# The passage from the gate stage to the dense stage: a first small store, eight early gathers, and the split of the token halves in the last routing head

## The chip, the cores and the metric

The kernel runs on one core of a Trainium2 chip. The metric is the device time of one execution in microseconds (us). A time `t` is counted from the start of the profiled execution's span. Engines: TensorE (PE, and PEld for its weight loads), VectorE (DVE), ScalarE (ACT), GpSimd (POOL), and SyncE (SP), which only issues DMAs here. Sixteen DMA engines serve two queues: q1, fed by SP, and q0, fed by GpSimd's indirect DMAs.

## The reference

Two layers over 640 tokens (512 latent, 128 context) of width 1024. Layer 0 mixes tokens by grouped-query attention, layer 1 by pooling. Each mixer is followed by a PEER channel mixer, which is where the change lies:

```
q  = (x @ wq) -> (t, 8 heads, 2 halves, 128);  sc = q . keys           # 128 keys per half
s_top, i_top = top_k(sc, 16)
cs, ci = top_k(s_top[0][:, None] + s_top[1][None, :], 16)              # 16 of 256 pairs
idx = i1 * 128 + i2;   g = softmax(cs)                                 # 16384 experts
act = gelu(u[idx] . x, exact) * g;   out = sum_k act_k * v[idx_k]      # per token: 8 x 16 experts
```

u and v have 16384 rows of 1024 numbers each, per layer, in float32.

## The kernel before, in words

**Two ways for the experts.** The 640 tokens are five tiles of 128. For three tiles (384 tokens, `TD`) the experts are computed densely: all 128x128 experts, 128 "key rows" q of 128 experts each, with a gate matrix that is zero where a token did not choose an expert. For the other two tiles (256 tokens, `NG`) the rows of u and v that each token chose are gathered by indirect DMA, 128 rows of 4 KB (0.524 MB) at a time, 256 of them in u and 256 in v per layer, and VectorE does the products. Both ways run at the same time, in the dense stage. "Expert q" below is such a key row of 128 experts.

**Stages of a layer's channel mixer.** (1) Routing: TensorE and ScalarE produce the scores of 16 half-heads; VectorE takes the top 16 head by head (`routing`, some 25.6 us a head); GpSimd multiplies and folds the masks of each head (lines 464 to 476). After the eighth head come the softmax of the gates, the row numbers `idx` (line 930) and the low half of the dense tokens, `hl = hT - hh` (line 933), where `hh` is ScalarE's rounding of `hT` (line 532). (2) Gate stage: three blocks of 128 tokens. For each, TensorE transposes the picks, VectorE copies them to `pickT` (942) and builds one-hot tiles `hot` for four tokens at a time (952), GpSimd multiplies one of the two by the gates (487), TensorE multiplies the pair (1106) and ScalarE copies the result to `gbuf` (541). `gbuf` has two halves of 64 tokens; SP stores each full half, 4 MB, into the scratch tensor `gates_d` in HBM (`store_gates`, 362), six stores per layer. (3) Dense stage, 16 groups of eight experts (`experts` on each engine): per expert a scan on TensorE (24 matmuls, lines 1118 to 1120: u in a high and a low half, `uh` and `ul`, against `hh` and `hl`), gelu on ScalarE (560), the product with the gate on VectorE (989, from `gp`, four key rows read back from `gates_d`), splits of v and of that product (`vh`, `vl`, `wh`, `wl`), and a spread on TensorE (18 matmuls, 1130 to 1132). TensorE runs scan q+1 ahead of spread q. Beside it VectorE does four gathered rows per expert: in the first eight groups dot products with u rows against the tokens `htok` (`u_row`, 970), in the last eight sums of v rows into `acc` (`v_row`, 979).

**The order around the change.** Every engine has its instructions in one fixed order. Between the last gate copy and the first scan: TensorE transposes the gathered tiles' tokens into PSUM, ScalarE splits two u tiles and then waits for the semaphore `dense_begun`. VectorE raises `dense_begun` (1008) only when both halves' last stores have landed (`stored[0]`, `stored[1]`), then clears `acc` (1009). Behind `dense_begun` stand: SP's loads, in the order gates 0 to 3, v pairs 0 and 1, gates 4 to 7; ScalarE's copies of `htok` (576); GpSimd's first gather (506). The ring of gathered rows has eight buffers (`rows`), free again when VectorE has used one. In the loop SP issues, per pair p of experts, `load_u(p+2)` when `ul` of that slot is made, `load_v(p+2)` when `vl` is, and every second pair the gates. The buffers of the dense stage overlay those of the routing and gate stages in SBUF, which is why the gathers and some loads wait for the stores.

## Time and profile before

| | us |
|---|---|
| median of three runs | 3490.77 (3490.72 to 3492.78) |
| the profiled execution's own time | 3486.53 |
| its span, first to last instruction | 3484.7 |
| TensorE busy (matmuls) | 3144.4 (90%) |
| VectorE busy | 2939.8 (84%) |
| GpSimd busy | 1897.1 (54%) |
| ScalarE busy | 1053.9 (30%) |
| DMA, mean over the span | 286 GB/s |

Busy times overlap, so they do not add up to the span. A mean share mixes stages: in the dense stages (t=801 to 1889 and 2367 to 3455) TensorE, VectorE and the DMA engines are all near full, in the routing stages only VectorE is. The granted TensorE clock is given as a share of full speed (1.00 is 2.4 GHz, 0.50 is 1.2 GHz). In a timeline row, the bracket at the end gives the idle time of the engine just before the row and what ended it.

### The profile page before, as it was taken

What the parts mean: (1) busy time and instruction counts of PE and PEld (TensorE: products, weight loads), DVE (VectorE), ACT (ScalarE), POOL (GpSimd) and SP (SyncE); (2) the same over time, 40 slices, a digit from 0 to 9 for tenths busy, and PEclk for the clock granted to TensorE, in tenths of its full rate; (3) what the DMA queues carried; (4) which work ended last, traced back from release to release, by engine and by line L of the source; (5) the groups of instructions that cost most, each with busy time, mean ns of one, the idle gap of its engine ahead of it and who ended that gap; (6) DMA issues with size and microseconds to landing.
All of it is one profiled execution on the core that took longest, in us unless ns stands there. A gap on an engine that the chain in (4) does not pass through costs nothing.

```text
span 3484.7 us, 50069 instructions
## 1 busy us (share of the span) xinstructions
PE 3144.4 (90%) x15686; PEld 2594.2 (74%) x15686; DVE 2939.8 (84%) x5453; ACT 1053.9 (30%) x1587; POOL 1897.1 (54%) x1412
## 2 busy tenths in 40 slices
PE   5988999398999999999998597298999999999997
PEld 3555555277999999899987264277999999999996
DVE  1655278897999999999998678896999999999998
ACT  2122111143333333333333210143333333333332
POOL 0000023485777887777774023485777777676673
PEclk8999999699999999999999798599999999999999
DMA  5122154048999999999997010048999999999995
GB/s 200 49 98 74 73 189 174 24 199 348 410 408 407 404 402 380 402 404 406 402 387 282 24 49 0 24 205 350 409 409 408 403 404 395 410 401 404 407 400 204
DMA packets 244633, 995.72 MB, mean 286 GB/s; under 512 B 22608, under 2 KB 72528, under 8 KB 204880
## 3 DMA queue, kind: packets, MB, share of 16 engines
q0 software_dynamic: 147456, 536.94, 39.0%
q1 hardware_dynamic: 97104, 457.82, 33.4%
q8 instruction: 45, 0.74, 0.1%
q14 instruction: 28, 0.23, 0.0%
HBM read 941.45 MB, written 53.22 MB: 285 GB/s over the span
## 4 chain that ended last, share of the span: by engine, by line
PE 64%; DVE 18%; issue 8%; DMA 7%; POOL 2%; ACT 1%; DVEq 0%; POOLq 0%; SPq 0%; ACTq 0%
PE bankA L1118 7%; PE bankA L1120 7%; PE bankA L1119 7%; PE bankD L1106 6%; PE bankD L1131 5%; PE bankD L1132 5%; PE bankD L1130 5%; PE bankA L1210 5%; DMA rows<-in_v,idxc 4%; DVE acc L979 3%; PE bankA L1132 2%; PE bankA L1131 2%; PE bankA L1130 2%; PE bankD L1256 2%; DMA rows<-in_u,idxc 1%
## 5 line engine op out<-in xcount | busy, mean ns | idle before, releaser
L506 POOL DMA_INDIRECT rows<-in_u,idxc x512 | 750.2, 1465 | 235.1 <-issue 129.4
L506 POOL DMA_INDIRECT rows<-in_v,idxc x512 | 688.0, 1344 | 252.1 <-issue 134.1
L1118 PE MATMUL bankA<-hh,uh 128*128 128x384 f32 x2048 | 689.8, 337 | 22.5 <-ACT htok L576 13.8
L1120 PE MATMUL bankA<-hh,ul 128*128 128x384 f32 x2048 | 689.6, 337 | 0.0
L1119 PE MATMUL bankA<-hl,uh 128*128 128x384 f32 x2048 | 688.2, 336 | 0.0
L979 DVE SCALAR_TENSOR_TENSOR acc<-rows,a,acc 128x1024 f32<-128x1024 f32 x512 | 634.6, 1278 | 15.9 <-DMA rows<-in_v,idxc 15.4
L970 DVE CUSTOM_DVE_ANT_0 rows<-rows,htok 128x1024 f32<-128x1024 f32 x512 | 607.1, 1219 | 21.0 <-DMA rows<-in_u,idxc 19.7
L468 POOL TENSOR_TENSOR mask<-mask,topf 128x1280 f32<-128x1280 f32 x32 | 91.9, 2893 | 875.0 <-DVE mask L898 875.0
L560 ACT ACTIVATE wt<-bankA 128x384 f32<-128x384 f32 x256 | 126.0, 492 | 971.7 <-PE bankA L1120 971.6
L1118 PEld LDWEIGHTS bankA<-hh,uh 128*128 128x128 f32 x2048 | 386.4, 189 | 34.5 <-ACT htok L576 14.5
L1131 PE MATMUL bankD<-vl,wh 128*128 128x512 f32 x1024 | 400.0, 391 | 0.0
L1132 PE MATMUL bankD<-vh,wl 128*128 128x512 f32 x1024 | 399.4, 390 | 0.0
L1130 PE MATMUL bankD<-vh,wh 128*128 128x512 f32 x1024 | 398.6, 389 | 0.0
L1210 PE MATMUL bankA<-hT,wch 128*128 128x512 f32 (+1 forms) x1344 | 377.9, 440 | 22.1 <-ACT hT L621 21.8
L1119 PEld LDWEIGHTS bankA<-hl,uh 128*128 128x128 f32 x2048 | 386.1, 189 | 9.7
L1120 PEld LDWEIGHTS bankA<-hh,ul 128*128 128x128 f32 x2048 | 385.9, 188 | 0.0
L1210 PEld LDWEIGHTS bankA<-hT,wch 128*128 128x128 f32 x1344 | 209.6, 194 | 191.2 <-issue 188.4
L991 DVE TENSOR_TENSOR vl<-vraw,vh 128x1024 fp32r<-128x1024 f32 x256 | 312.3, 1220 | 32.2 <-ACT vh L564 31.7
L963 DVE TENSOR_TENSOR ul<-uraw,uh 128x1024 fp32r<-128x1024 f32 x256 | 311.8, 1219 | 9.2 <-ACT uh L550 9.2
L564 ACT CAST vh<-vraw 128x1024 fp32r<-128x1024 f32 x256 | 266.5, 1041 | 11.6 <-DMA vraw<-in_vP 11.6
L550 ACT CAST uh<-uraw 128x1024 fp32r<-128x1024 f32 x256 | 268.6, 1050 | 0.0
L566 ACT CAST wh<-wt 128x384 fp32r<-128x384 f32 x256 | 131.4, 513 | 403.9 <-DVE wt L989 403.7
(178 smaller groups left out, 4589.9 us busy)
## 6 DMA issues: line engine op xcount, KB each, us to landing
uraw<-in_uT SPq DMA_DIRECT2D x128, 1024.0 KB, 16.2
vraw<-in_vP SPq DMA_DIRECT2D x128, 1024.0 KB, 7.9
gates_scratch<-gbuf SPq DMA_DIRECT2D x12, 4096.0 KB, 11.6
gp<-gates_scratch SPq DMA_DIRECT2D x64, 768.0 KB, 16.3
sq<-in_ada SPq DMA_DIRECT2D x14, 2048.0 KB, 8.0
wch<-in_ada SPq DMA_DIRECT2D x10, 2048.0 KB, 8.0
wch<-in_wq SPq DMA_DIRECT2D x8, 2048.0 KB, 8.1
rows<-in_u,idxc POOLq DMA_INDIRECT x512, 9.8
```

The lines of the kernel that those rows point to most:

```text
L506: pool.indirect_dma_start(out=rows[:, j, :], out_offset=None, in_=table.rearrange("l e d -> (l e) d"), in_offset=bass.IndirectOffsetOnAxis ...
L963: v.tensor_tensor(ul[:, c, :], uraw[:, b, c * D:(c + 1) * D], uh[:, c, :].bitcast(F32), ALU.subtract).then_inc(ul_ready, 1)
L970: v.tensor_tensor_reduce(out=rows[:, r % RING, :], in0=rows[:, r % RING, :], in1=htok[:, r % GT, :], scale=1.0, scalar=0.0, op0=ALU.mult, ...
L979: v.scalar_tensor_tensor(out=acc[:, r % GT, :], in0=rows[:, r % RING, :], scalar=a8[:, r:r + 1], in1=acc[:, r % GT, :], op0=ALU.mult, op1= ...
L991: v.tensor_tensor(vl[:, c % 2, :], vraw[:, b, c % 2 * D:(c % 2 + 1) * D], vh[:, c % 2, :].bitcast(F32), ALU.subtract).then_inc(vl_ready, 1)
L1118: pe.matmul(abank[c], hi, hh[:, k, :], start=k == 0, stop=False)
L1119: pe.matmul(abank[c], hi, hl[:, k, :], start=False, stop=False)
L1120: last = pe.matmul(abank[c], lo, hh[:, k, :], start=False, stop=k == K - 1)
L1130: pe.matmul(y, hi, vh[:, c, a:a + 512], start=first, stop=False)
L1131: pe.matmul(y, hi, vl[:, c, a:a + 512], start=False, stop=False)
L1132: last = pe.matmul(y, lo, vh[:, c, a:a + 512], start=False, stop=final)
L1210: last = pe.matmul(bank[:, a:b], w[:, k, (c % 4) * P:(c % 4 + 1) * P], hT[:, k, a:b], start=k == 0, stop=k == K - 1)
```

## The change

Four edits.

1. `hl` is computed by GpSimd instead of VectorE, between the seventh and the eighth head's masks. ScalarE makes `hh` before it waits for the softmax, and TensorE transposes the gathered tiles' tokens (`htok`) before it waits for the gates; ScalarE's copies follow at once.
2. The last block's second half is stored in two parts: its first eight key rows (256 KB, semaphore `edge_stored`), and the rest later. `dense_begun` waits for the copies into `gbuf` and for the first half's store alone. SP's order becomes: first part of the store, v pair 0, (wait for the first part) gates 0 to 3, v pair 1, rest of the store, u pair 2, (wait for the rest) gates 4 to 7, and on as before.
3. GpSimd issues the first eight gathers in the gate stage: three after block 1, three after block 2, two after block 3. For this five of the eight row buffers lie over `hT` and three in a tile of their own, and other dense tiles change places.
4. `acc` is cleared between the u rows and the v rows, in the middle of the dense stage.

```diff
@@ SBUF
-            hh = sb("hh", [P, K, TD], F32R, where=dn)
-            hl = sb("hl", [P, K, TD], F32R, where=dn)
+            htok = sb("htok", [P, GT, D], where=dn)
             uraw = sb("uraw", [P, 2, 2 * D], where=dn)
+            rowsB = sb("rowsB", [P, RING - TILES, D], where=dn)
...
-            rows = sb("rows", [P, RING, D], where=dn)
-            htok = sb("htok", [P, GT, D], where=dn)
-            acc = sb("acc", [P, GT, D], where=dn)
+        hrows = hT[:, :, :].rearrange("p k t -> p (k t)").rearrange("p (r d) -> p r d", d=D)
+        row_buf = [hrows[:, j, :] if j < TILES else rowsB[:, j - TILES, :] for j in range(RING)]
+        htok_bank = [bankA[0], bankD[1]]
@@ SP
-                    sp.dma_start(gates_d[b], gbuf[:, b % 2, :, :]).then_inc(stored[b % 2], 16)
+                    if b < TD // TB - 1:
+                        sp.dma_start(gates_d[b], gbuf[:, b % 2, :, :]).then_inc(stored[b % 2], 16)
+                    else:
+                        sp.dma_start(gates_d[b][:, 0:GROUP, :], gbuf[:, b % 2, 0:GROUP, :]).then_inc(edge_stored, 16)
+
+            def store_rest(L):
+
+                b = TD // TB - 1
+                sp.dma_start(gates_d[b][:, GROUP:NKEY, :], gbuf[:, b % 2, GROUP:NKEY, :]).then_inc(stored[b % 2], 16)
...
                             load_u(L, g * (GROUP // 2) + (p + 2), p % 2)
+                            if first and p == 0:
+                                sp.wait_ge(stored[1], 16 * ((L + 1) * DT + 1))
+                                load_gates(4, 1)
...
                 sp.wait_ge(dense_begun, L + 1)
+                load_v(L, 0, 0)
+                sp.wait_ge(edge_stored, 16 * (L + 1))
                 load_gates(0, 0)
-                load_v(L, 0, 0)
                 load_v(L, 1, 1)
-                load_gates(4, 1)
-                with sp.Fori(0, GROUPS - 1) as g:
+                store_rest(L)
+                group(0, first=True)
+                with sp.Fori(1, GROUPS - 1) as g:
                     group(g)
@@ GpSimd
+                with pool.Fori(0, PH - 1) as h:
+                    pick_keys(h)
+                pool.wait_ge(split_h, L + 1)
+                pool.tensor_tensor(hl[:, :, :], hT[:, :, 0:TD], hh[:, :, :].bitcast(F32), ALU.subtract
+                                   ).then_inc(h_split, 1)
+                pick_keys(PH - 1)
+                pool.wait_ge(idx_ready, L + 1)
+                pool.wait_ge(h_split, L + 1)
+                pool.wait_ge(htok_full, (L + 1) * GT)
+                pool.tensor_copy(idxc[:, 0, :], idx[:, 0:RING]).then_inc(idx_copied, 1)
...
+                for i in range(1, DT + 1):
                     pool.wait_ge(pickT_ready, i + L * DT)
...
                                 ALU.mult).then_inc(hotg_ready, 1)
-                pool.wait_ge(idx_ready, L + 1)
-                pool.wait_ge(dense_begun, L + 1)
...
+                    for j in range(3 * i - 3, min(3 * i, RING)):
+                        gather(u_d, j, 0)
@@ ScalarE
+                act.copy(hh[:, :, :], hT[:, :, 0:TD]).then_inc(split_h, 1)
+                for j in range(GT):
+                    act.wait_ge(htok_full, L * GT + j + 1)
+                    act.copy(htok[:, j, :], htok_bank[j][:, :]).then_inc(htok_ready, 1)
                 act.wait_ge(gexp_in, L + 1)
@@ VectorE
-                v.wait_ge(split_h, L + 1)
-                v.tensor_tensor(hl[:, :, :], hT[:, :, 0:TD], hh[:, :, :].bitcast(F32), ALU.subtract).then_inc(h_split, 1)
...
+                v.wait_ge(g_out, (L + 1) * DT * (P // HOT) + 2)
+                v.wait_ge(stored[0], 16 * ((L + 1) * DT + 1))
+                v.sem_inc(dense_begun, 1)
                 for c in range(2):
                     split_u(L * NKEY + c, 0, c)
-                v.wait_ge(g_out, (L + 1) * DT * (P // HOT) + 2)
-                for i in range(2):
-                    v.wait_ge(stored[i], 16 * ((L + 1) * DT + 1))
-                v.sem_inc(dense_begun, 1)
-                then(v.memset(acc[:, :, :], 0.0))
...
                 v.sem_inc(u_done, 1)
+                v.wait_ge(stored[1], 16 * ((L + 1) * DT + 1))
+                then(v.memset(acc[:, :, :], 0.0))
@@ TensorE
+                pe.wait_ge(a_free, BEFORE[L])
+                pe.wait_ge(sc_copied, HP * (L + 1))
+                for j in range(GT):
+                    for m in range(K):
+                        last = pe.transpose(htok_bank[j][:, m * P:(m + 1) * P], hT[:, m, (DT + j) * P:(DT + j + 1) * P], ident)
+                    last.then_inc(htok_full, 1)
                 pe.wait_ge(routed, L + 1)
```

## Rows read from the trace of the kernel before

**Rows 1.** Stretches: length, busy us (instructions) by engine, granted clock, DMA share, GB/s.
```profile
801.00:850.00 49.00, 34.85 (x166) 30.63 (x164) 25.49 (x35) 14.86 (x20) 21.94 (x20) 0.90 0.92 369
850.00:900.00 50.00, 49.46 (x250) 44.93 (x251) 48.58 (x75) 17.38 (x24) 34.94 (x27) 1.00 1.03 407
...
1369.00:1889.00 520.00, 517.37 (x2605) 468.47 (x2603) 500.79 (x506) 177.92 (x247) 377.77 (x277) 1.00 0.99 389
```
**Rows 2.** TensorE's waits, 801 to 870: total us, times, longest.
```profile
PE bankA L1118 <- ACT htok L576: 6.9, 1, 6.9
PE bankA L1118 <- DVE ul L963: 5.2, 3, 3.0
PE bankA L1130 <- DVE wl L994: 2.6, 2, 1.8
```
**Rows 3.** The chain of waits over both passages: start us, us, what.
```profile
800.76 13.04 DMA gates_scratch<-gbuf
...
829.30 18.70 DMA rows<-in_u,idxc
...
850.54 0.41 PE bankA L1118
...
2367.34 13.04 DMA gates_scratch<-gbuf
...
2416.57 0.41 PE bankA L1118
```
**Rows 4.** The same chain, end of layer 0's routing.
```profile
672.49 3.27 DVE hl L933
675.75 0.22 DVE bankA L937
```
**Rows 5.** Timeline, GpSimd's masks of head 6 and ScalarE's softmax exponent.
```profile
631.27 5.72 POOL L468 TENSOR_TENSOR mask<-mask,topf 128x1280 f32<-128x1280 f32 x2 [16.69 <-DVE mask L898]
...
668.61 0.74 ACT L530 ACTIVATE gt<-gt 128x640 f32<-128x640 f32 x1 [47.78 <-DVE gt L917]
```
**Rows 6.** Timeline of layer 0's passage.
```profile
803.29 2.36 DVE L963 TENSOR_TENSOR ul<-uraw,uh 128x1024 fp32r<-128x1024 f32 x2 [3.52 <-ACT uh L550]
...
813.98 1.01 ACT L576 COPY htok<-bankA 128x1024 f32<-128x1024 f32 x1 [9.85 <-DVEq L1008]
...
814.50 1.76 DVE L1009 MEMSET acc<- 128x2048 f32 x1 [8.85 <-DMA gates_scratch<-gbuf]
...
819.05 0.56 DVE L989 TENSOR_TENSOR wt<-wt,gp 128x384 f32<-128x384 f32 x1 [2.78 <-DMA gp<-gates_scratch]
...
821.89 1.05 ACT L564 CAST vh<-vraw 128x1024 fp32r<-128x1024 f32 x1 [5.59 <-DMA vraw<-in_vP]
...
824.81 0.47 PE L1130 MATMUL bankA<-vh,wh 128*128 128x512 f32 x1 [1.76 <-DVE wl L994]
```
**Rows 7.** Timeline, first work after the change from block 1 to block 2.
```profile
720.96 4.42 POOL L487 TENSOR_TENSOR hot<-hot,pickT 128x512 f32<-128x512 f32 x4 [4.42 <-DVE hot L952]
...
722.05 3.20 PE L1106 MATMUL bankD<-hot 128*128 128x128 f32 x16 [3.98 <-POOL hot L487]
```
**Rows 8.** A stretch behind that idle time, columns as in rows 1.
```profile
724.00:726.00 2.00, 2.00 (x11) 2.00 (x11) 1.72 (x3) 0.78 (x2) 1.81 (x3) 0.50 1.22 524
```
**Rows 9.** DMA issues of the page: count, KB each, us to landing.
```profile
out_yT<-hT SPq DMA_DIRECT2D x8, 320.0 KB, 2.4
```
**Rows 10.** DMA queues in 822 to 830: packets, MB, share of 16 engines.
```profile
q0 software_dynamic: 557, 2.02, 63.6%
q1 hardware_dynamic: 551, 1.20, 38.8%
```
**Rows 11.** Line 506, the gathers' issue on GpSimd: ns min/median/max.
```profile
L506 POOL DMA_INDIRECT rows<-in_u,idxc x512: 937/1307/1992, 815.6 to 2906.9; - x171
L506 POOL DMA_INDIRECT rows<-in_v,idxc x512: 934/1202/4019, 1343.3 to 3437.1; - x171
```
**Rows 12.** Timeline, VectorE between the u rows and the v rows.
```profile
1355.24 0.45 DVE L1020 TENSOR_TENSOR actg<-actg,gate 128x256 f32<-128x256 f32 x1 [0.80 <-ACT actg L581]
```

More of the change, by code:

```diff
@@ L213, in build @@
                     sq = sb("sq", [P, K, T], where=wide)
-                with ExitStack() as gb:
-                    pickT = sb("pickT", [P, 3, P], where=gb)
-                    hot = sb("hot", [P, SLOTS, 2, HOT, P], where=gb)
-                    gbuf = sb("gbuf", [P, 2, NKEY, TB], where=gb)
             QT, OT = qT[:, 0:NH, :], qT[:, NH:2 * NH, :]
@@ L237, in build @@
                 gsum = sb("gsum", [P, TILES * PH], where=rt)
+                pickT = sb("pickT", [P, 3, P], where=rt)
+                hot = sb("hot", [P, SLOTS, 2, HOT, P], where=rt)
+                gbuf = sb("gbuf", [P, 2, NKEY, TB], where=rt)
             with ExitStack() as pl:
@@ L377, in expert_loads, with group @@
             def expert_loads(L):
-                def group(g, last=False):
+                def group(g, first=False, last=False):
                     for p in range(GROUP // 2):
@@ L477, in _, with gather, gather_ring @@
                     last.then_inc(mask_done, 1)
-                with pool.Fori(1, DT + 1) as i:
+                def gather(table, slot, g):
+                    pool.indirect_dma_start(
+                        out=row_buf[slot], out_offset=None, in_=table.rearrange("l e d -> (l e) d"),
+                        in_offset=bass.IndirectOffsetOnAxis(ap=idxc[:, g % 2, slot:slot + 1], axis=0),
+                    ).then_inc(row_ready[slot], 16)
+                def gather_ring(table, i, it, g):
+                    pool.wait_ge(rows_free, it * ROWS + (g * RING + 1))
+                    rows_of = bass.ds(i * ROWS + g * RING, RING) if not isinstance(i, int) else slice(
+                        i * ROWS + g * RING, i * ROWS + (g + 1) * RING)
+                    pool.tensor_copy(idxc[:, g % 2, :], idx[:, rows_of]).then_inc(idx_copied, 1)
+                    pool.wait_ge(idx_copied, it * (ROWS // RING) + (g + 1))
+                    pool.sem_inc(pool_passed, 1)
+                    for j in range(RING):
+                        pool.wait_ge(rows_free, it * ROWS + (g * RING + j + 1))
+                        pool.sem_inc(pool_passed, 1)
+                        gather(table, j, g)
+                with pool.Fori(0, PH - 1) as h:
[8 more added lines that the diff above has]
+                pool.tensor_copy(idxc[:, 0, :], idx[:, 0:RING]).then_inc(idx_copied, 1)
+                pool.wait_ge(idx_copied, L * 2 * ITERS * (ROWS // RING) + 1)
+                pool.wait_ge(rows_free, L * 2 * ITERS * ROWS + RING)
+                for i in range(1, DT + 1):
                     pool.wait_ge(pickT_ready, i + L * DT)
-                    pool.sem_inc(pool_passed, 1)
                     with pool.Fori(0, P // HOT // SLOTS) as k:
@@ L573, in experts @@
                 act.wait_ge(dense_begun, L + 1)
-                for j in range(GT):
-                    act.wait_ge(htok_full, L * GT + j + 1)
-                    act.copy(htok[:, j, :], ybank[j][:, :]).then_inc(htok_ready, 1)
                 with act.Fori(0, ITERS) as g:
@@ L1140, in group @@
                         spread(q, c % 2, first and c == 0, last and c == GROUP - 1)
-                for j in range(GT):
-                    for m in range(K):
-                        last = pe.transpose(ybank[j][:, m * P:(m + 1) * P], hT[:, m, (DT + j) * P:(DT + j + 1) * P], ident)
-                    last.then_inc(htok_full, 1)
                 pe.wait_ge(h_split, L + 1)
```

47 lines of the change are left out of this document (23 added, 24 removed).

## The prediction

> **What bounds the kernel now.** I read the stretches table first, then TensorE's waits, then the chain of waits over the two passages, and last the timeline around each edited step. Each layer has a routing stage on VectorE, a gate stage (three blocks of 128 tokens), and a dense stage of 128 experts that takes some 1060 of the layer's 1700 us. In the dense stage TensorE is busy 517.4 of 520 us in the second half of layer 0, while the 16 DMA engines are busy 0.99 of that time at 389 GB/s, and 1.03 at 407 GB/s in the 50 us after t=850 [rows 1]. So the body is set by TensorE with DMA right behind it; 2605 matmuls in 517.4 us are 0.199 us each, and the 42 of one expert (24 of the scan, 18 of the spread) take 8.3 us. Nothing in the change touches this body. What it touches is the way in: between t=801 and 850 TensorE is busy 34.9 of 49 us. Its waits there are 6.9 us for the token copy htok, 5.2 us for ul and 2.6 us for wl [rows 2]. The chain says what stands behind them: the last 4 MB gate store takes 13.04 us from t=800.76, with everything held behind it, and then the first row gathers arrive late (18.70 us for one), so that the scan of expert 4 starts at 850.54, 49.8 us after the last store's issue. In layer 1 it is 2367.34 to 2416.57, 49.2 us [rows 3]. From there on TensorE hardly stops. The start of scan 4 is therefore my landmark: what the change wins up to there, it keeps, if DMA lets it.
>
> **Part 1, the token halves.** Before, the split's difference hl is on the chain for 3.27 us on VectorE, between the expert numbers and the gate stage [rows 4]. It moves to GpSimd, ahead of the last head's masks. GpSimd idles 16.69 us before each head's masks and does a 1280-element pair product in 2.86 us (5.72 for two) [rows 5]; 3072 elements at that rate are 6.9 us. It starts when head 6's masks are done and fits more than twice, so even a doubled price costs nothing. Its input, ScalarE's copy hh, and the two htok copies (1.01 us each) move into the 47.78 us for which ScalarE stood idle before the softmax exponent [rows 5]. TensorE's 16 transposes for htok go into its idle time there as well. Gain 3.3 us a layer, all on the chain; what is late next is pickT, which waits for nothing else. If the cover were gone, each us of excess over 16.7 would cost one.
>
> **Part 2, the passage.** I keep the trace's own times and take the 3.3 us off at the end. Unchanged: the casts uh on ScalarE, then ul on VectorE at 803.29 (two in 2.36 us), so scan 0 starts at 804.66 [rows 6]. TensorE then has been idle since 800.2, 4.5 us, because the transposes that stood there are gone. After an idle time of 3.98 us at a block's change [rows 7] the granted clock was 0.50 in 724 to 726, the 1.2 GHz level [rows 8], and about 3.4 us of half speed cost 1.7 us of work. I charge that: scan 0 ends at 804.66+4.15+1.7 = 810.5, scan 1 at 814.65.
> For spread 0 there have to be: the gates of experts 0 to 3, vraw, and the chain gelu, wt, vh, vl, wl. Only 8 key rows (256 KB) are stored first; a 320 KB store lands in 2.4 us [rows 9], so at 803.2. The read-back took 5.0 us (813.98 to 819.05, where wt started as it landed) [rows 6]; with the 1 MB of vraw ahead of it in SP's queue (2.6 us at 407 GB/s) it lands at 810.9. vraw, issued at 801.1, needed 7.5 us before (landed 821.89) [rows 6] and is there at 808.6. Gelu ends at 811.0, then vh 1.05, vl 1.22, wl 0.55: 813.9. So spread 0 starts behind scan 1 at 814.65, against 824.81 before [rows 6].
> From there the experts follow without a gap if the rows are in place: eight are, for experts 0 and 1. Spread 0 ends at 818.8, then scan 2, spread 1, scan 3, spread 2 at 4.15 each: scan 4 at 835.4 against 850.54. That is 15.1 us, the best that TensorE can do.
> The DMA engines give the other bound. From 801 to 850 they moved 49 x 369 = 18.1 MB [rows 1], 4.2 of it the store, so 13.9 MB of dense data by the landmark. Now six gathers (3.15 MB of 0.524 each) came earlier, but 4.2 MB of store go inside: 14.9 MB at 407 GB/s are 36.6 us, plus some 2 us before the first data, from 801: 839.6, 10.9 us won. The need is not strict, since some of the 13.9 MB was ahead of its use. I take the middle of 10.9 and 15.1, 13.0 us.
> SP's queue in this passage: behind its new wait for the rest of the store stand the second gate load, vraw pair 2, then uraw pair 3. The rest (3.9 MB) is issued at about 804 behind 2.8 MB of loads and lands near 824 (its predecessor's 13.04 us from 811). The gates of experts 4 to 7 and vraw pair 2 are needed at 844 and 845, and uraw pair 2, issued ahead of the wait but moved behind the rest, at 833: covered by 7 us or more. If that cover is gone TensorE waits at scan 4.
>
> The trace shows how the two queues share an engine: in 822 to 830 the gathers' queue moved 557 packets and SP's 551, yet 2.02 and 1.20 MB [rows 10]; they alternate by packet, not by byte. The Trainium skill ("DMA: Bandwidth & Descriptors", Queues, rings and completion order) says the same: an engine takes a whole packet from one ring before it goes to the next. The trace agrees. It speaks against this change, as gbuf is stored in runs of 30 KB a partition and a row is 4 KB: by it, gathers issued from 815 on stand nearly still until the store's rest is through near 822, and if that made scan 4 some 2 us later, the sum would be 3464.
>
> **Part 3, gathers in the gate stage.** Eight indirect DMAs go on GpSimd's queue: three after block 1, three after block 2, two after block 3. GpSimd idles 4.42 us at a block's change [rows 7]. An issue lasts 0.94 us at least, 1.31 in the median of the dense stage, plus 0.3 to the next [rows 11]: three are 3.7 to 4.8 us. Two changes cost 0 to 0.4 us each, and I take 0.5 a layer for them and the index copy. The last two follow the last product, where nothing waits. The gathers' own buffers (five of eight now over hT, three behind uraw) wait only for the split and the transposes, long done. The DMA engines were half idle there, so the data is free.
>
> **Part 4, the cleared accumulator.** Its 1.76 us [rows 6] stood in the passage's idle time and go to the middle of the dense stage, ahead of the product with the gate, which waited 0.80 us for ScalarE anyway [rows 12]. VectorE loses 1.0 us once a layer; TensorE had no wait there. From 0 to 1.0, I take 0.3.
>
> **The sum.** Per layer 3.3+13.0-0.5-0.3 = 15.5; two layers 31.0, less 0.6 for layer 1's shorter passage: 30.4. The profiled span of 3484.7 becomes 3454.3, its own time 3486.5 about 3456, and since the median of the runs is 4.2 above that execution's, 3460 us.
>
> **The rivals.**
> 1. DMA is the bound, at the 369 GB/s of the old passage and not at 407: the gathers of the second ring land behind the store's rest, and scan 4 waits for its rows as before. 14.9 MB then take 40.4 us, scan 4 starts at 841.4, 9.1 us won. For it: DMA is 1.03 busy behind the old passage too. Against: TensorE was busy 49.5 of 50 us in 850 to 900 on that supply [rows 1]. 3.3+9.1-0.8 = 11.6 a layer, 22.6 with layer 1's 0.6: 3468 us.
> 2. TensorE is the bound and all cover holds: 3.3+15.1 = 18.4 a layer less the 0.6: 3454.6 us. For it: eight rows ready, against 6.9 us of htok waiting gone; against: the store's 4.2 MB are on top.
> 3. Slower: the gathers hold up the gate stage. GpSimd's issue can last 4.02 us (the longest in the trace, against a median of 1.20) [rows 11]. Three at 4.02+0.3 are 13.0, 8.5 beyond the idle 4.42; TensorE, starved, restarts at the 0.50 clock for 1.7 more: 10.2 a change, 20.4 a layer, against 16.3 won: 4.1 lost, 3499 us. It decides from 3.9 us an issue. Against it: the medians, 1.20 and 1.31 us.
> 4. The passage gives nothing, because what is won is waited for again in the dense stage (SP's loads lapse by the rest of the store, each buffer late for the next); only hl stays: 3484 us. Against it: DMA moved 407 GB/s where an expert needs 3.34 MB in 8.3 us (0.52 each of u and v, 0.20 of gates, four rows of 0.52), 403: small debts are paid back.
>
> **How the numbers follow.** Forecast 0.55, rival 1 0.24, rival 2 0.13, rival 3 0.03, rival 4 0.05. The range takes in rivals 1 and 2 and the bounds of the clock (up to 1.7 more a layer) and of the gate read-back: 3449 to 3473. Under 0.2% (7 us) a measurement of this kernel can't tell a change. Faster is the sum of forecast and rivals 1 and 2, 0.92; within 0.2% rival 4, 0.05; slower rival 3, 0.03.
>
> **What would show it.** In the profile after: no hl on the chain, gate stage 3.3 us earlier; GpSimd's idle at a block's change replaced by three issues and TensorE's gap still near 4 us; no gate store on the chain at the passage; scan 0 partly at 0.50; spread 0 some 14 us after the last gate copy (24.1 before); scan 4 37 us after the last store's issue, not 49.8; TensorE gapless behind it. Rows or the second gates awaited before scan 4 would mean rival 1; block gaps of 8 us and more rival 3. The prediction is wrong if the landmark moves and the dense stage grows by as much.

## The result and the profile after

The changed kernel takes 3465.71 us (median of six runs, 3459.17 to 3468.66) against 3489.26 (3485.68 to 3492.78, six runs): a ratio of 0.9932 [0.9919, 0.9945], or 23.6 us less by the medians, between 19 and 28 by the interval. Forecast were 3460.0 us and 3449 to 3473. The profiled execution of after took 3468.56 us with a span of 3466.7, which is 18.0 less than the span of before. The stretches that answer to [rows 1], in the same columns:
```profile
801.00:850.00 49.00, 44.33 (x214) 41.09 (x215) 36.99 (x55) 17.50 (x24) 24.94 (x19) 0.93 0.99 389
850.00:900.00 50.00, 47.05 (x234) 41.69 (x233) 43.76 (x67) 15.80 (x22) 29.90 (x26) 1.00 1.02 397
1369.00:1889.00 520.00, 513.86 (x2579) 464.23 (x2578) 497.71 (x505) 178.27 (x247) 371.26 (x271) 0.99 0.98 383
```
TensorE is 9.5 us busier in the 49 us of the passage, and 2.4 us less busy in the 50 us behind it, where before it hardly stopped. The third row seems to show 3.5 us less in the v half, but its stretch is fixed and the dense stage now ends earlier: its last matmul ends at 1882.5, before at 1888.8. Up to these ends TensorE is idle for 3.4 us after and for 2.4 before; the rest lies behind the dense stage.

The waits in 801 to 870, to be held against [rows 2] (waits in all, times, longest):
```profile
PE bankA L1167 <- DVE ul L1004: 4.6, 1, 4.6
PE bankA L1179 <- DVE wl L1035: 1.3, 1, 1.3
DVE wt L1030 <- DMA gp<-gates_scratch: 9.4, 1, 9.4
POOL idxc L511 <- DVE a L1011: 19.5, 3, 17.1
```
The token copy is gone from the list, and what TensorE waited for shrank from 14.7 to 5.9 us. VectorE's wait for the gate read-back grew from 2.8 us to 9.4. GpSimd waits 17.1 us in front of the second ring's index copy, until VectorE has used the first row; before, it waited 15.5 us for `dense_begun`, in front of the first ring's. The chain of waits shows the same by its pieces, for [rows 3, 4]:
```profile
678.89 1.05 POOL hot L539
...
800.55 5.83 DMA gates_scratch<-gbuf
...
806.39 8.35 DMA gp<-gates_scratch
...
837.23 14.03 DMA hT<-in_u,idxc
...
855.66 17.93 DMA hT<-in_u,idxc
...
2361.89 4.27 DMA gates_scratch<-gbuf
...
2366.18 7.70 DMA gp<-gates_scratch
```
The split hl is on it no more, and the 13.04 us store is replaced by a small store and the read-back. Two row gathers, issued at 837.23 and 855.66, are on it, and both land behind the landmark: scan 4 starts at 837.89, which is 37.3 us after the edge store's issue ("edge store" is the small first store), and in layer 1 35.1 us after it. The forecast was 37.

**A ruler for all kernels.** From the timelines I took six events in each layer: VectorE's candidate adds of the last head, GpSimd's first gate product, SP's issue of the last block's first gate store (where a kernel has none, VectorE's copy of these gates), and ScalarE's gelu of experts 4, 16 and 127. The gelus of expert 4 and 16 in layer 0, first of before and then of after:
```profile
855.00 0.49 ACT L560 ACTIVATE wt<-bankA 128x384 f32<-128x384 f32 x1 [0.35 <-PE bankA L1120]
...
954.85 0.49 ACT L560 ACTIVATE wt<-bankA 128x384 f32<-128x384 f32 x1 [3.07 <-PE bankA L1120]
```
```profile
842.27 0.49 ACT L606 ACTIVATE wt<-bankA 128x384 f32<-128x384 f32 x1 [1.92 <-PE bankA L1169]
...
945.60 0.49 ACT L606 ACTIVATE wt<-bankA 128x384 f32<-128x384 f32 x1 [2.44 <-PE bankA L1169]
```
The differences between these events, in us, layer 0 / layer 1:

| kernel | head to gate stage | gate stage | passage, to gelu 4 | gelu 4 to 16 | median |
|---|---|---|---|---|---|
| before | 34.9 / 34.8 | 121.7 / 122.0 | 54.2 / 53.7 | 99.9 / 100.0 | 3489.26 |
| after | 34.1 / 33.9 | 121.7 / 122.0 | 41.7 / 39.5 | 103.3 / 102.7 | 3465.71 |
| e1 hl on VectorE | 34.8 / 34.8 | 122.0 / 122.0 | 40.5 / 40.2 | 102.4 / 104.5 | 3465.22 |
| e2 hl in pieces | 34.6 / 34.5 | 122.2 / 122.5 | 40.5 / 40.9 | 102.2 / 104.0 | 3465.52 |
| e3 rest cut | 34.1 / 34.0 | 122.8 / 122.7 | 40.7 / 38.9 | 99.7 / 99.7 | 3459.31 |
| e4 gathers late | 34.1 / 34.0 | 121.6 / 122.2 | 46.9 / 47.6 | 102.9 / 102.3 | 3475.56 |
| e5 two halves | 31.5 / 31.5 | 121.7 / 121.9 | 43.5 / 41.0 | 100.9 / 102.9 | 3458.32 |
| e6 gathers 2-3-3 | 34.1 / 33.9 | 121.6 / 122.7 | 40.2 / 38.9 | 102.3 / 102.1 | 3458.59 |
| e7 gates on chip | 34.1 / 34.0 | 122.7 / 122.1 | 38.9 / 39.4 | 101.8 / 102.4 | 3456.98 |
| e8 gates before v | 34.1 / 34.0 | 122.6 / 122.7 | 41.1 / 43.0 | 103.5 / 102.3 | 3465.33 |
| e9 halves, 2-3-3 | 31.6 / 31.5 | 122.1 / 122.4 | 39.5 / 38.8 | 101.3 / 102.0 | 3452.30 |
| e10 PE kept busy | 31.6 / 31.6 | 121.8 / 122.4 | 37.4 / 37.4 | 104.2 / 102.5 | 3452.68 |
| e11 all | 31.6 / 34.8 | 121.9 / 123.1 | 37.3 / 37.3 | 101.8 / 101.8 | 3453.33 |
| e12 all, mended | 31.6 / 31.6 | 121.9 / 122.5 | 37.3 / 37.3 | 101.7 / 102.0 | 3452.95 |

Twelve experts without a gap take 99.7 us (e3's rows; 12 x 8.31), so what the fourth column has above that is time given back behind the landmark. The stretch from gelu 16 to 127 is 922.0 in layer 1 before and 922.1 after; in layer 0 it was 924.7 before and 928.6 after, and 922.0 or 922.1 in seven experiments. No other trace has more than the 924.7 of before, so the 3.9 us is most likely this execution's own. Before itself has 2.7 us above 922.0, after 6.5, and the largest piece of these 6.5 can be seen. Near 1490 VectorE waits three times for gathered v rows (1.1, 1.1 and 0.5 us), and then TensorE stops:
```profile
1495.88 0.47 PE L1179 MATMUL bankA<-vh,wh 128*128 128x512 f32 x1 [1.84 <-DVE wl L1035]
```
Behind this stop the granted clock is 0.57 from 1496 to 1500, and the experts 82 and 83 take 3.9 us more than two others. Why these rows came late stays open. By the columns, layer 0 won 0.8 + 0.1 + 12.5 - 3.5 = 9.9 and layer 1 0.9 + 0.0 + 14.2 - 2.6 = 12.5; less the 3.9 that is 18.5, against 18.0 in the spans, and without it 22.4, near the 23.6 of the medians.

How finely may the columns be read? The gate stage is between 121.6 and 123.1 us in all of these traces, though TensorE's gaps at the changes of block are 3.98 us in nearly all of them. What differs is how long the granted clock then stands at 0.50: some 3.4 us in some executions and 6.8 in others. The same holds in the passage: 6.8 us in both layers of after, 3.4 in both of e5. Half speed for 3.4 us more costs up to 1.7 us, so a difference of under 2 us in one column of one trace is not a finding by itself.

**The switches between gate blocks.** After, in answer to [rows 7]:
```profile
716.13 1.14 POOL L501 DMA_INDIRECT hT<-in_u,idxc  x1 [0.17 <-issue]
...
718.82 0.94 POOL L501 DMA_INDIRECT hT<-in_u,idxc  x1 [0.30 <-issue]
720.40 3.28 POOL L539 TENSOR_TENSOR hot<-hot,pickT 128x512 f32<-128x512 f32 x3 [0.64 <-DVE hot L993]
```
```profile
721.49 3.78 PE L1155 MATMUL bankD<-hot 128*128 128x128 f32 x17 [3.98 <-POOL hot L539]
```
Three issues fill GpSimd's idle time and leave 0.64 us of it; TensorE's gap is 3.98 us, as before.

**The passage of layer 0**, for [rows 6]; SP, GpSimd and the compute engines by their decisive rows:
```profile
800.55 0.33 SPq L371 DMA_DIRECT2D gates_scratch<-gbuf  x1
...
806.39 0.40 SPq L387 DMA_DIRECT2D gp<-gates_scratch  x1
...
807.42 0.45 SPq L376 DMA_DIRECT2D gates_scratch<-gbuf  x1
```
```profile
804.38 0.66 PE L1167 MATMUL bankA<-hh,uh 128*128 128x384 f32 x1 [4.56 <-DVE ul L1004]
...
814.77 0.56 DVE L1030 TENSOR_TENSOR wt<-wt,gp 128x384 f32<-128x384 f32 x1 [9.40 <-DMA gp<-gates_scratch]
...
817.08 0.47 PE L1179 MATMUL bankA<-vh,wh 128*128 128x512 f32 x1 [1.30 <-DVE wl L1035]
...
820.17 1.02 POOL L501 DMA_INDIRECT hT<-in_u,idxc  x1 [0.91 <-POOL idxc L511]
...
873.03 0.41 PE L1167 MATMUL bankA<-hh,uh 128*128 128x384 f32 x1 [1.75 <-DVE ul L1004]
...
878.22 0.47 PE L1179 MATMUL bankA<-vh,wh 128*128 128x512 f32 x1 [0.79 <-DVE wl L1035]
```
Scan 0 starts on time. The read-back can't be issued before 806.39, since the 256 KB store ahead of it takes 5.83 us. From spread 0 at 817.08 TensorE has no gap until 873.03. The first gather of the second ring is issued at 820.17, and the queues show what it meets. In 815 to 820 SP's queue moved 79 packets and 2.14 MB, and GpSimd's none; then, in 820 to 825 (packets, MB, share of 16 engines):
```profile
q1 hardware_dynamic: 146, 1.91, 89.2%
q0 software_dynamic: 19, 0.08, 3.8%
```
All 19 of the gathers' packets fall behind 824. When nothing else was under way, the first packets came 1.4 us after a gather's issue (716.13), here some 4 us after it. The granted clock (third from the end, before DMA share and GB/s) stood at 0.50, the 1.2 GHz level, after TensorE's idle 4.56 us, from 804 to 810:
```profile
806.00:808.00 2.00, 2.00 (x7) 2.00 (x7) 0.00 (x0) 0.00 (x0) 0.00 (x0) 0.50 0.84 311
```

### The profile page after: what moved, and what is told of

Its sections match the earlier page's. It is cut to its first block, busy times and chain, and to the rows that moved or that the text cites. A ratio compares the mean times of both kernels' runs of the same rounds, so it can differ in the third digit from the quotient of the medians.

```text
span 3466.7 us, 49891 instructions
## 1 busy us (share of the span) xinstructions
PE 3146.5 (91%) x15686; PEld 2596.1 (75%) x15686; DVE 2936.6 (85%) x5451; ACT 1056.1 (30%) x1587; POOL 1890.6 (55%) x1414
## 4 chain that ended last, share of the span: by engine, by line
PE 64%; DVE 19%; issue 8%; DMA 6%; POOL 2%; ACT 1%; DVEq 1%; POOLq 0%; SPq 0%; ACTq 0%
PE bankA L1169 8%; PE bankA L1167 8%; PE bankA L1168 8%; PE bankD L1180 5%; PE bankD L1181 5%; PE bankD L1179 5%; PE bankA L1254 5%; PE bankD L1155 5%; PE bankA L1181 3%; PE bankA L1180 3%; PE bankA L1179 3%; DVE acc L1020 2%; PE bankD L1300 2%; DMA hT<-in_v,idxc 2%; PE bankA L1246 1%
## 5 line engine op out<-in xcount | busy, mean ns | idle before, releaser
L501 POOL DMA_INDIRECT hT<-in_v,idxc x320 | 452.5, 1414 | 187.8 <-issue 65.2
L501 POOL DMA_INDIRECT hT<-in_u,idxc x320 | 446.2, 1394 | 176.3 <-issue 72.2
L1020 DVE SCALAR_TENSOR_TENSOR acc<-hT,a,acc 128x1024 f32<-128x1024 f32 x320 | 399.5, 1277 | 16.6 <-DMA hT<-in_v,idxc 16.0
L1011 DVE CUSTOM_DVE_ANT_0 hT<-hT,htok 128x1024 f32<-128x1024 f32 x320 | 382.1, 1219 | 20.2 <-DMA hT<-in_u,idxc 17.8
L1032 DVE TENSOR_TENSOR vl<-vraw,vh 128x1024 fp32r<-128x1024 f32 x256 | 311.8, 1218 | 18.5 <-ACT vh L610 14.5
L501 POOL DMA_INDIRECT rowsB<-in_u,idxc x192 | 285.7, 1488 | 62.6 <-issue 59.2
L501 POOL DMA_INDIRECT rowsB<-in_v,idxc x192 | 233.5, 1216 | 70.7 <-issue 54.3
## 6 DMA issues: line engine op xcount, KB each, us to landing
gates_scratch<-gbuf SPq DMA_DIRECT2D x10, 4096.0 KB, 11.6
```

What stands on the lines that cost most here:

```text
L501: pool.indirect_dma_start(out=row_buf[slot], out_offset=None, in_=table.rearrange("l e d -> (l e) d"), in_offset=bass.IndirectOffsetOnAxis ...
L1011: v.tensor_tensor_reduce(out=row_buf[r % RING], in0=row_buf[r % RING], in1=htok[:, r % GT, :], scale=1.0, scalar=0.0, op0=ALU.mult, op1=AL ...
L1020: v.scalar_tensor_tensor(out=acc[:, r % GT, :], in0=row_buf[r % RING], scalar=a8[:, r:r + 1], in1=acc[:, r % GT, :], op0=ALU.mult, op1=ALU ...
L1032: v.tensor_tensor(vl[:, c % 2, :], vraw[:, b, c % 2 * D:(c % 2 + 1) * D], vh[:, c % 2, :].bitcast(F32), ALU.subtract).then_inc(vl_ready, 1)
```

## The experiments

Two questions stood open: why the gate stage starts only 0.9 us earlier and not 3.3, and what takes back 3.5 and 2.6 us behind gelu 4. The edits are against the changed kernel; all were run in five rounds, and each ratio is to the kernel before on the same chip. e1 to e4 ran on one chip, e5 to e8 on a second, e9 to e11 on a third, e12 on a fourth, so medians of different groups are to be compared by their ratios. On the second chip the kernel before ran anywhere from 3482 to 3496 us, which makes the ratios of e5 to e8 the least certain.

**e1: hl on VectorE again.**
```diff
-                pool.wait_ge(split_h, L + 1)
-                pool.tensor_tensor(hl[:, :, :], hT[:, :, 0:TD], hh[:, :, :].bitcast(F32), ALU.subtract
-                                   ).then_inc(h_split, 1)
# on VectorE, behind the expert numbers idx
+                v.wait_ge(split_h, L + 1)
+                v.tensor_tensor(hl[:, :, :], hT[:, :, 0:TD], hh[:, :, :].bitcast(F32), ALU.subtract).then_inc(h_split, 1)
```


> The changed kernel with one edit undone: hl is computed by VectorE again, behind the expert numbers. Theory (port): in the changed kernel GpSimd's 6.65 us hl blocks VectorE's two-source adds into cand (3.20 us in place of 0.69), so the move won 3.3 us and lost 2.4 us a layer. Then here the last head takes 25.6 us again in place of 28.1, the cand group 0.69 us, hl is on the chain for 3.3 us, and the time is 0.9 us a layer longer than the changed kernel's 3465.7: about 3467.5. Rival (the last head is longer for another reason, such as ScalarE's or TensorE's earlier work): the last head stays at 28 us and the time is 3.3 us a layer longer, 3472.

Measured: 3465.22 us, 0.9939 [0.9925, 0.9952]. To be seen in the rows are the same four small adds, first in after, where GpSimd's hl is under way, and then in e1, where it is not there:
```profile
640.83 6.65 POOL L522 TENSOR_TENSOR hl<-hT,hh 128x3072 fp32r<-128x3072 f32 x1
...
644.64 0.28 DVE L901 FIND_INDEX8 topi<-top,sc 128x8 uint32<-128x128 f32 x1
644.84 3.20 DVE L905 TENSOR_TENSOR cand<-top 128x80 f32<-128x80 f32 x4
```
```profile
644.85 0.70 DVE L902 TENSOR_TENSOR cand<-top 128x80 f32<-128x80 f32 x4
...
673.04 3.35 DVE L973 TENSOR_TENSOR hl<-hT,hh 128x3072 fp32r<-128x3072 f32 x1
```
In after the adds end at 648.0, half a microsecond behind hl's end at 647.5: they stand still for 2.5 us until GpSimd has finished, and the head's chain with them. That 2.5 us of the 3.35 is lost again is the whole answer to the first question (head to gate stage 34.9 before, 34.1 after, 34.8 here). The index searches on VectorE run beside hl at their old speed, 0.28 us each; of what ran beside it only the adds, which read two operands from SBUF (the on-chip memory), stopped. The Trainium skill ("SBUF — State Buffer", Who interferes with whom) has it as a rule: an instruction of VectorE with two inputs in SBUF and one of GpSimd that reads SBUF share a port, and the later one waits for the whole of the earlier. The trace agrees, by 3.20 us against 0.70. The medians of e1 and after can't be told apart, as 0.8 us a layer would let one expect.

**e2: hl in eight pieces**, so that an add waits for a piece only.
```diff
-                pool.tensor_tensor(hl[:, :, :], hT[:, :, 0:TD], hh[:, :, :].bitcast(F32), ALU.subtract
-                                   ).then_inc(h_split, 1)
+                for m in range(K):
+                    piece = pool.tensor_tensor(hl[:, m, :], hT[:, m, 0:TD], hh[:, m, :].bitcast(F32), ALU.subtract)
+                piece.then_inc(h_split, 1)
```


> The changed kernel with hl on GpSimd in eight instructions of 384 elements in place of one of 3072. Theory (port, held for a whole instruction): VectorE's cand adds wait at most for one piece (0.85 us) at a time, so the cand group shrinks from 3.20 us to between 0.7 and 2 us, and the time falls by 1 to 2.4 us a layer: 3461 to 3464. Rival (the port is shared by bandwidth, so both are slowed for as long as GpSimd works): the cand group stays near 3 us and the time at 3465.7 or above.

Measured: 3465.52 us, 0.9939 [0.9926, 0.9953]. The pieces brought nothing; GpSimd's row and VectorE's:
```profile
642.63 7.66 POOL L523 TENSOR_TENSOR hl<-hT,hh 128x384 fp32r<-128x384 f32 x8
```
```profile
646.62 3.78 DVE L906 TENSOR_TENSOR cand<-top 128x80 f32<-128x80 f32 x4
```
A piece takes 0.96 us and there are four adds, each of which meets one: 4 x 0.96 = 3.8. Each add gets in as soon as one piece ends, but the next add then meets the next piece. That the wait is the number of adds times the length of a piece agrees with the port theory, though the gain I looked for here was not there.

**e5: hl in two halves around the adds.** The second half waits until VectorE has passed them.
```diff
+                pool.tensor_tensor(hl[:, 0:K // 2, :], hT[:, 0:K // 2, 0:TD], hh[:, 0:K // 2, :].bitcast(F32), ALU.subtract)
+                pool.wait_ge(step, (98, 237)[L] + 11 * (PH - 1) + 4)
+                pool.tensor_tensor(hl[:, K // 2:K, :], hT[:, K // 2:K, 0:TD], hh[:, K // 2:K, :].bitcast(F32), ALU.subtract
+                                   ).then_inc(h_split, 1)
```


> The changed kernel with hl on GpSimd in two halves of 1536 elements: the first straight after head 6's masks (while VectorE runs its max and index searches), the second only when VectorE is past head 7's cand adds. Theory (the port is held per instruction, and only VectorE's instructions with two sources are kept out; the eight pieces lost time because each of the four cand adds met one piece): the cand group takes 0.69 us, the last head 25.7 us, and hl costs nothing: 2.4 us a layer less than the changed kernel on the trace up to the gate stage, 4.8 us in all. Rival (any GpSimd work beside VectorE slows its searches too): the last head stays over 27 us.

Measured: 3458.32 us, 0.9910 [0.9895, 0.9924]. VectorE's adds, and GpSimd's two halves on either side:
```profile
643.90 0.69 DVE L907 TENSOR_TENSOR cand<-top 128x80 f32<-128x80 f32 x4
```
```profile
639.89 3.42 POOL L522 TENSOR_TENSOR hl<-hT,hh 128x1536 fp32r<-128x1536 f32 x1
...
647.33 3.42 POOL L524 TENSOR_TENSOR hl<-hT,hh 128x1536 fp32r<-128x1536 f32 x1 [4.02 <-DVE csv L918]
```
Head to gate stage falls to 31.5 us in both layers: 3.3 below before, the term of the prediction in full. The passage is longer than after's, though (43.5 and 41.0): the edge store was again held up, for 6.0 and 5.7 us.

**e3: the store's rest cut down** from 3840 to 256 KB. This kernel leaves out the gates of 112 key rows of the last 64 dense tokens; other numbers stand there, written once in layer 0's routing (lines not shown).
```diff
-                sp.dma_start(gates_d[b][:, GROUP:NKEY, :], gbuf[:, b % 2, GROUP:NKEY, :]).then_inc(stored[b % 2], 16)
+                sp.dma_start(gates_d[b][:, GROUP:2 * GROUP, :], gbuf[:, b % 2, GROUP:2 * GROUP, :]).then_inc(stored[b % 2], 16)
```


> The changed kernel with the rest of the last store cut from 3840 KB to 256 KB: 112 of the 128 key rows of the last 64 dense tokens hold other numbers, written once in layer 0's routing. Theory (DMA debt): what the passage wins is partly given back behind expert 4 (TensorE 3.7 us in layer 0, 2.6 us in layer 1), because 3.6 MB of store, 9 us at 407 GB/s, go ahead of the second ring of gathers. Then here the give-back disappears: 6 us less than the changed kernel, about 3459, and VectorE's waits for gathered u rows fall from 8.5 us to under 3 in layer 0. Rival (the gathers lag because GpSimd issues them one by one only when rows come free, whatever DMA does): give-back and time as in the changed kernel, 3465.

Measured: 3459.31 us, 0.9929 [0.9915, 0.9942], 6 us less than e1 and e2 on the same chip. Gelu 4 to 16 is 99.7 us in both layers, with no gap. TensorE's waits from 817 to 1369, in e3 and then in after:
```profile
PE bankA L1185 <- DVE wl L1041: 1.6, 1, 1.6
```
```profile
PE bankA L1179 <- DVE wl L1035: 2.5, 3, 1.3
PE bankA L1167 <- DVE ul L1004: 1.8, 1, 1.8
```
e3's one wait is that of spread 0; after's are that one (1.3) and the gaps at 873, 878 and 887. So what is given back is the price of the rest's 3.6 MB: data that before was moved while TensorE stood, and now has to be moved while it works. Whether it is the bytes as such or the place of these large packets ahead of the gathers, e3 does not tell apart. The passage itself (40.7 and 38.9) is as in after within 1 us, so up to gelu 4 the rest does not hold it up. This answers the second question.

**e4: all eight gathers behind the gate stage.**
```diff
-                    for j in range(3 * i - 3, min(3 * i, RING)):
-                        gather(u_d, j, 0)
+                pool.wait_ge(dense_begun, L + 1)
+                for j in range(RING):
+                    gather(u_d, j, 0)
```


> The changed kernel with the first eight gathers issued behind the gate stage, when the dense stage has begun, and all else as it is. Theory (DMA bytes): six gathers, 3.15 MB or 7.7 us of DMA at 407 GB/s, go back into the passage, so the landmark (expert 4's scan) comes some 6 to 8 us later per layer, near 3479. Rival (TensorE's chain over the gates is the bound, and rows are first needed 16 us after the last gate copy): under 2 us a layer, 3467 to 3470.

Measured: 3475.56 us, 0.9974 [0.9964, 0.9984].
```profile
800.64 0.33 SPq L371 DMA_DIRECT2D gates_scratch<-gbuf  x1
...
802.94 0.40 SPq L387 DMA_DIRECT2D gp<-gates_scratch  x1
```
```profile
818.42 0.56 DVE L1031 TENSOR_TENSOR wt<-wt,gp 128x384 f32<-128x384 f32 x1 [12.96 <-DMA gp<-gates_scratch]
```
Without gathers ahead of it the edge store takes 2.3 us, the figure of [rows 9]. But then the read-back runs beside the gathers and takes 15.5 us, and gelu 4 comes 5 and 8 us later than in after. By the columns passage and gelu 4 to 16 together the early gathers are worth 4.7 + 7.7 = 12.4 us (the medians say 9.9, the ratios 14.6), and without them 8.1 us of the gain over before is left.

**e6: gathers 2-3-3**, two ahead of the first block and none behind the last.
```diff
+                for j in range(2):
+                    gather(u_d, j, 0)
...
-                    for j in range(3 * i - 3, min(3 * i, RING)):
+                    for j in range(3 * i - 1, min(3 * i + 2, RING)):
```


> The changed kernel with the eight early gathers issued two before block 1, three after block 1 and three after block 2, none after block 3. Theory (the last two gathers, 1.05 MB, stand before the small first store on the DMA engines): the first store lands 2.3 us after its issue, as in the run with late gathers, in place of 5.83 and 4.27 us; the gates' read-back starts 3.5 and 2 us earlier, so spread 0 comes up to 2.3 us earlier until scan 0 and 1 bound it. 3 to 4 us less in all. Rival (the read-back with v pair 0 ahead of it is the bound): spread 0 moves by under 1 us.

Measured: 3458.59 us, 0.9914 [0.9899, 0.9930].
```profile
798.80 0.33 SPq L371 DMA_DIRECT2D gates_scratch<-gbuf  x1
...
800.96 0.40 SPq L387 DMA_DIRECT2D gp<-gates_scratch  x1
```
```profile
810.54 0.56 DVE L1032 TENSOR_TENSOR wt<-wt,gp 128x384 f32<-128x384 f32 x1 [6.92 <-ACT wt L608]
```
The store takes 2.16 us (2.17 in layer 1), the gates are there before gelu, and spread 0 follows scan 1 without a gap. So the two gathers issued at 798.75 and 800.09 in after are what held the store for 5.83 us. The passage is 1.5 and 0.6 us shorter, and all four columns together are 3.0 us shorter than in after; the medians differ by 7.1. For e5 and e7 it is 3.9 and 3.6 against 7.4 and 8.7. The traces do not show where the rest comes from; the unsteady kernel before on this chip makes it doubtful.

**e7: the last block's gates of experts 0 to 3 copied on chip**, by VectorE from gbuf; the other blocks' are read back in the gate stage. The small first store goes, and the last store is whole again, behind v pair 1 (these lines are not shown).
```diff
+                sp.dma_start(gp[0][:, 0:TD // TB - 1, :, :].rearrange("p b i t -> p b (i t)"),
+                             gates_d[0:TD // TB - 1, :, 0:4, :].rearrange("b p i t -> p b (i t)")
+                             ).then_inc(gp_ready[0], 16)
...
+                then(v.tensor_copy(gp[0][:, TD // TB - 1, :, :], gbuf[:, 1, 0:4, :]))
```


> The changed kernel without the small first store: the first four key rows of the first five 64-token blocks are read back while the last block is still being computed, and VectorE copies the last block's four key rows from gbuf to gp0 (128x256 numbers, about 0.3 us); the last store goes out whole after v pairs 0 and 1. Theory (the gates' path over HBM, 14.2 us in layer 0, sets spread 0): the first product with the gates waits for gelu alone, at some 10.5 us after the last gate copy, spread 0 some 14 us after it in place of 16.5, and scan 4 2.4 us earlier; some of it given back as DMA debt. 3 to 5 us less in all. Rival (v pair 0 or TensorE's slow scans are right behind): under 1 us.

Measured: 3456.98 us, 0.9908 [0.9893, 0.9924].
```profile
800.81 0.48 DVE L1048 COPY gp<-gbuf 128x256 f32<-128x256 f32 x1 [1.10 <-ACT gbuf L588]
...
811.23 0.56 DVE L1031 TENSOR_TENSOR wt<-wt,gp 128x384 f32<-128x384 f32 x1 [5.64 <-ACT wt L607]
```
With no trip to memory on the path, the passage is 38.9 and 39.4 us: 2.8 shorter than after's in layer 0, 0.1 in layer 1. The wait for gp was worth no more than that; in layer 0 the clock also stood at 0.50 for 3.4 us only, against 6.8 in after.

**e8: the read-back ahead of the v pair in SP's queue.**
```diff
-                load_v(L, 0, 0)
                 sp.wait_ge(edge_stored, 16 * (L + 1))
                 load_gates(0, 0)
+                load_v(L, 0, 0)
                 load_v(L, 1, 1)
```


> The changed kernel with SP's read-back of gates 0 to 3 ahead of v pair 0. Theory (the queue's order): the read-back takes 5 us as in the kernel before and not 8.35, so wt starts 3 us earlier, but v pair 0, issued 5 us later, then lands last, near 13 us after the last copy; spread 0 moves by 1 to 2 us, 2 to 3 us less in all. Rival: v pair 0 becomes the later of the two and the time is 0 to 3 us longer.

Measured: 3465.33 us, 0.9931 [0.9916, 0.9946], not to be told from after. In layer 1 the read-back took 4.9 us, but the passage 43.0. The v pair is now the later one:
```profile
813.83 1.05 ACT L610 CAST vh<-vraw 128x1024 fp32r<-128x1024 f32 x1 [2.66 <-DMA vraw<-in_vP]
...
816.75 0.47 PE L1179 MATMUL bankA<-vh,wh 128*128 128x512 f32 x1 [1.95 <-DVE wl L1035]
```

**e9: e5 and e6 together.**

> Two mends together: hl in two halves around VectorE's cand adds, and the eight early gathers two, three and three ahead of the last block. Theory: their gains stand at different places (end of routing, passage) and add up: 4.8 us and 6 us less than the changed kernel's 3465.7 on the trace's own terms, some 3455. Rival (DMA debt takes the second's gain, since the gathers' bytes are the same): 3459 as either alone.

Measured: 3452.30 us (3450.30 to 3455.09), 0.9905 [0.9888, 0.9921], span 3450.7. Both effects stand in the table side by side (31.6 and 39.5; 31.5 and 38.8). It has the lowest median of the study, 13.4 us below the change as it was; by the ratios (0.9905 against 0.9932) it is 9, and the columns say 9.6. By the ratios alone it can't be told from e5, e6 or e7; that it is ahead of each rests on the columns.

**e10: e9 and 32 transposes of the identity** on TensorE between the last gate product and scan 0.
```diff
                 pe.wait_ge(g_out, (L + 1) * DT * (P // HOT) + 2)
+                for m in range(32):
+                    pe.transpose(bankA[0][:, m % K * P:(m % K + 1) * P], ident, ident)
```


> As e9_halves_2_3_3, and TensorE fills its 4.5 us of idle time before scan 0 with 32 transposes of the identity into PSUM that nothing reads (some 3.5 us). Theory (clock): TensorE's idle time is what lets the granted clock fall to 0.50 in the passage, which stretches scan 0 from 4.1 to about 6 us; kept busy, scan 0 ends 1.5 to 2 us earlier and with it gelu 0 and spread 0, unless v pair 0 or the gates are then awaited: 1 to 3 us less in all than e9_halves_2_3_3. Rival (gates or v land later than scan 0 anyway): no change in spread 0.

Measured: 3452.68 us, 0.9907 [0.9888, 0.9926]. The first row is e9's, the second e10's:
```profile
804.00:806.00 2.00, 2.00 (x8) 2.00 (x8) 0.00 (x0) 0.00 (x0) 0.00 (x0) 0.50 1.17 351
```
```profile
804.00:806.00 2.00, 2.00 (x14) 2.00 (x13) 0.06 (x1) 0.00 (x0) 0.00 (x0) 1.00 0.95 296
```
The clock stays at 1.00, the 2.4 GHz level, and the passage is 2.1 and 1.4 us shorter. But gelu 4 to 16 grows by 2.9 and 0.5 us, and the time is the same: 3.5 us won, 3.4 given back. That it is the DMA engines that take it back, as in e3, is likely, but no run shows it for this case. In e9 the clock stood at 0.50 for 6.8 us in layer 0 and for 3.4 in layer 1, which fits the larger gain in layer 0.

**e11: e7, e9 and e10 together.**

> Everything together: hl in two halves, gathers two-three-three, first gates read back in the gate stage with VectorE's copy of the last block's four key rows, TensorE kept busy in the passage. Theory: the gates are off the passage, scan 0 runs at the 2.4 GHz level, spread 0 starts some 12.5 us after the last gate copy (16.5 in the changed kernel), and 0.65 MB less of DMA stand in the dense stage's start: 3450 to 3454. Rival (DMA debt behind expert 4 takes all of what the passage wins more): as e9_halves_2_3_3 within 1 us.

Measured: 3453.33 us, 0.9911 [0.9892, 0.9930]; within 1.1 us of e9, as its rival had it. In layer 1 head to gate stage was 34.8, because e7's copy adds a step to VectorE's count and the second half of hl was let go one step early.

**e12: the same with that count mended** (237 becomes 238).

> As e11 (halves, gathers 2-3-3, gates of the last block taken on chip, 32 transposes as filler), but in layer 1 the second half of hl waits one VectorE step later. In e11 the copy that was added on VectorE counts one step, so in layer 1 the second half started at 2193.69 against VectorE's reduction and not behind its adds, and from the last head's candidate adds to the first gate product it took 34.75 us (31.59 in layer 0). Port theory: 31.6 in both layers, the other stretches as in e11, so 3.2 us less: span near 3448.8, median near 3450. Rival (the DMA debt takes whatever the passage or the stage before it wins): the gate stage starts 3.2 us earlier and the stretch from gelu 4 to gelu 16 grows from 101.8 to about 105, median 3453.

Measured: 3452.95 us (3451.22 to 3454.00), 0.9902 [0.9886, 0.9919]. The stage is 31.6 us in both layers and gelu 4 to 16 stays 101.7 and 102.0, so on that stretch the port theory held and the debt did not grow. Yet the median is that of e9 and e11 (by the ratios 0.9902, 0.9905 and 0.9911, well within their intervals): gelu 16 to 127 took 923.9 and 923.2 us where these two had 922.1 and 922.0, and layer 1's last head began 332.9 us after layer 0's last gelu (331.0 in e9, 331.3 in e11). Differences of 1 to 3 us in stretches that the edit doesn't touch come with each profiled execution; three versions at 3452 to 3453 can't be ranked.

## Why the prediction was right in direction and too good by 6 us

- **Part 1, hl: the mis-sized term, 3.3 forecast, 0.8 and 0.9 measured.** The step that failed reads "it starts when head 6's masks are done and fits more than twice, so even a doubled price costs nothing". GpSimd's duration was right (6.65 us for 6.9), its idle time too. I asked only whether GpSimd had time, and not what VectorE does beside it: four adds of 0.70 us in all became 3.20. e1 and e2 show it by taking the cause away and by cutting it up, e5 by moving it: the forecast gain comes back in full. In two layers the mistake is 4.9 us.
- **Part 2, up to scan 4: 13.0 forecast; 12.5 and 14.2 measured at gelu 4.** That this number fits so well is luck, for two errors nearly cancelled. The edge store was put at 2.4 us, the row of [rows 9], which stood alone on its queue; here it was issued behind two gathers and took 5.83 and 4.27 (e4, e6: 2.2 to 2.3 without them). My own part 3 had moved them there. The read-back behind the v pair was put at 7.7 us and took 8.35 and 7.70. So spread 0 came 16.5 us after the edge store's issue instead of 13.9. Against that, the forecast took the middle between TensorE's and DMA's bound, and up to gelu 4 TensorE's held: from 817.08 it had no gap, and five times 4.15 us later scan 4 was due at 837.8; gelu 4 at 842.3 is that plus its scan.
- **Part 2, behind scan 4: the DMA bound came late, not never.** "What the change wins up to there, it keeps, if DMA lets it": it did not, for 3.5 and 2.6 us. Net of that the passage gave 9.0 and 11.6, close to the 10.9 of the DMA bound and to rival 1's 9.1. The landmark sat too early for a bound by bytes. e3 shows that the rest of the store is the debt. In two layers it is 6.1 us, the second mis-sized term, put at nothing in the forecast. Rival 4 in its full form is excluded: it had the whole gain given back.
- **The clock: charged 1.7 us; e10 gives 2.1 and 1.4** at the passage. What it did not buy is time at the end.
- **The queues' rule held in its outcome.** The Trainium skill's rule that I cited ("DMA: Bandwidth & Descriptors", Queues, rings and completion order) had gathers nearly standing still behind the 30 KB runs. The trace agrees in the outcome: nothing in 815 to 820, 0.08 MB in 820 to 825. The alternation itself these rows do not show: in 820 to 825 SP's queue moved 146 packets and the gathers' 19, and from 822 on SP's were mostly of 8 KB. The prediction's 2 us a layer by that rule is of the size of the 3.5 and 2.6 found, and these were paid behind gelu 4, since eight rows were ready; that the rule is their cause is not shown.
- **Part 3, gathers at the switches: 0.5 forecast, nothing measured** (gate stage 121.7 and 122.0 in both kernels, TensorE's gap 3.98 in both). Rival 3 is out; its price was also mis-worked, since with the 1.7 us a change that it charges it decides from 3.3 us an issue and not from 3.9. e4 prices the early gathers at 10 to 15 us in the whole.
- **Part 4, the accumulator: 0.3 forecast, nothing measured:** gelu 16 to 127 of layer 1, in which it lies, is 922.0 before and 922.1 after.
- **The sum.** With the measured terms: 0.85 x 2 + 9.0 + 11.6 = 22.3 instead of 30.4, against 23.6 in the medians. The 8.1 us between 30.4 and 22.3 are 4.9 of hl and 6.1 of debt, less 1.3 by which the passage up to gelu 4 did better and 1.6 that parts 3 and 4 had charged. The distance in the result is smaller, 5.7 us, in part because the forecast started from a median of 3490.77 of three runs, and six give 3489.26.

## What to carry to other kernels

Moving work to an idle GpSimd needs two looks: whether it has the time, and whether what VectorE does meanwhile reads two operands from SBUF; place the moved work between such instructions, as e5 does. A small transfer on the critical path must not be issued behind large ones, even if these are on another queue, as the gathers were here; move the large ones earlier or later. And when bytes are taken out of an idle passage and put beside busy work, look for the gain some ten experts further on before it is booked, for a bound by DMA shows up only once the rows in store are used up.

## What was not expected of the hardware

- VectorE's two-operand adds wait for the end of a GpSimd instruction: 3.20 us for 0.70 beside one of 6.65 us, 3.78 beside eight of 0.96. Its index searches beside the same instruction kept their 0.28 us.
- A 256 KB store issued beside two row gathers of 512 KB took 5.83 and 4.27 us (6.0 and 5.7 in e5), and 2.1 to 2.3 without them. The read-back of 768 KB took 15.5 us beside the eight gathers (e4) and 8.35 behind a 1 MB load.
- 32 small transposes (3.72 us in all) in TensorE's idle time held the clock at 1.00, where it stood at 0.50 for 6.8 and 3.4 us in the same places of e9; measured in two layers, worth 2.1 and 1.4 us to the passage and nothing to the kernel's time.
- After the same idle time of TensorE (4.56 us in front of scan 0) the clock stood at 0.50 for 3.4 us in some executions and for 6.8 in others. This alone moves a passage by up to 1.7 us.
